# A projection by Strassen's seven products in three passes, with values and output gates turned later

## The reference, cut to what matters

```
xn   = rms_norm(x, g_norm);  proj = xn @ w_in          # 2112 x 1024 x 8200
q,k,v,o,z (1024 each), i,f (4 each), b,c,xc,z_cv (512 each), qx,zx (512 each) = split(proj)
h    = mlstm_chunkwise(q, k/16, v, i + b_i, log_sigmoid(f + b_f))   # 4 heads x 256
y_ml = rms_norm(sigmoid(o) * h, g_head) * silu(z)
y_cv = b * conv3(c * xc) * silu(z_cv)                   # also gives the conv state
y_xa = softmax(qx @ mem_k^T / sqrt(128)) @ mem_v * silu(zx)
out  = rms_norm(x + concat(y_ml, y_cv, y_xa) @ w_out, g_final)
```

## Time and profile before

| | us |
|---|---|
| median of 3 runs | 2346.0 (2344.82 to 2348.57) |
| the profiled execution | 2348.49 |
| its span, first to last instruction | 2346.7 |
| prep | 0 to 69.0 |
| project, first to last matmul | 69.0 to 1572.1 |
| attend | 1577.4 to 1882.9 |
| recur | 1882.9 to 2346.7 |
| PE busy | 2276.5 (97%) |
| mean granted clock of TensorE | 0.988 |

### The profile page before, as it was taken

How to read it: one execution, slowest core, us unless ns; L and a number is a source line. 1 busy time by engine, 2 the same in 40 slices (tenths; PEclk the granted TensorE clock), 3 DMA queues, 4 the chain that set the end, 5 groups by cost and what they waited for, 6 DMA issues and landing times. The chain is left out here.

```text
span 2346.7 us, 30090 instructions
## 1 busy us (share of the span) xinstructions
PE 2276.5 (97%) x11540; PEld 2021.2 (86%) x11540; DVE 694.2 (30%) x1524; ACT 435.4 (19%) x1000; POOL 177.9 (8%) x301
## 2 busy tenths in 40 slices
PE   7999999999999999999999999998999969999998
PEld 4899999999999999888888888987877858888885
DVE  7202323323001011011010333224334435555554
ACT  7110000001111111111111101113333222332231
POOL 0001000000100002300000000000000022222220
PEclk9999999999999999999999999999999989999999
DMA  7321101101122122222121255226445457677653
GB/s 271 86 81 42 51 8 52 45 14 66 49 85 90 49 84 83 53 78 75 57 83 45 83 75 58 99 75 213 162 123 158 153 155 218 186 221 210 197 164 82
DMA packets 237740, 245.40 MB, mean 105 GB/s; under 512 B 51000, under 2 KB 186976, under 8 KB 237616
## 3 DMA queue, kind: packets, MB, share of 16 engines
q1 hardware_dynamic: 193600, 164.17, 24.8%
q10 hardware_dynamic: 37648, 66.54, 8.4%
q0 software_dynamic: 6368, 12.96, 1.9%
HBM read 158.76 MB, written 84.85 MB: 104 GB/s over the span
## 5 line engine op out<-in xcount | busy, mean ns | idle before, releaser
L575 PE MATMUL bank<-xh,wh 128*128 128x424 f32 (+1 forms) x1640 | 581.0, 354 | 6.2 <-DVE wl L537 5.7
L577 PE MATMUL bank<-xh,wl 128*128 128x424 f32 (+1 forms) x1640 | 580.7, 354 | 0.0
L576 PE MATMUL bank<-xl,wh 128*128 128x424 f32 (+1 forms) x1640 | 580.6, 354 | 0.0
L575 PEld LDWEIGHTS bank<-xh,wh 128*128 128x128 f32 x1640 | 308.7, 188 | 16.0 <-DVE wl L537 8.2
L575 PE MATMUL bank<-wh,xh 128*128 128x512 f32 x816 | 317.6, 389 | 1.6 <-DVE wl L537 0.9
L576 PE MATMUL bank<-wl,xh 128*128 128x512 f32 x816 | 317.4, 389 | 0.0
L577 PE MATMUL bank<-wh,xl 128*128 128x512 f32 x816 | 317.4, 389 | 0.0
L576 PEld LDWEIGHTS bank<-xl,wh 128*128 128x128 f32 x1640 | 309.4, 189 | 5.5
L577 PEld LDWEIGHTS bank<-xh,wl 128*128 128x128 f32 x1640 | 308.9, 188 | 4.5
L545 DVE CAST wh<-raw 128x512 fp32r<-128x512 f32 (+1 forms) x136 | 55.8, 412 | 797.0 <-PE bank L577 792.1
L575 PEld LDWEIGHTS bank<-wh,xh 128*128 128x128 f32 x816 | 153.2, 188 | 34.0 <-DVE wl L537 2.3
(11 more groups left out here) (249 smaller groups left out, 2437.3 us busy)
## 6 DMA issues: line engine op xcount, KB each, us to landing
raw<-in_w_in SPq DMA_DIRECT2D x128, 256.0 KB, 4.0
scr_tm<-stage ACTq DMA_DIRECT2D x96, 256.0 KB
raw<-scr_qk SPq DMA_DIRECT2D x16, 1024.0 KB, 6.7
area<-scr_tm SPq DMA_DIRECT2D x32, 512.0 KB, 5.9
scr_qk<-stage ACTq DMA_DIRECT2D x48, 212.0 KB
xin<-in_x_prompt SPq DMA_DIRECT2D x16, 512.0 KB, 4.2
x_res<-in_x_prompt SPq DMA_DIRECT2D x16, 512.0 KB, 3.4
scr_acc<-x_res SPq DMA_DIRECT2D x16, 512.0 KB, 5.6
```

Of the source, the lines that this page charges most:

```text
L575: pe.matmul(out, ah, bh, start=(k == 0), stop=False)
L576: pe.matmul(out, ah, bl, start=False, stop=False)
L577: mm = pe.matmul(out, al, bh, start=False, stop=(k == KD - 1))
```

## The change

The projection's token-major and chunked groups are replaced by one scheme. The 2112 tokens are taken in three passes of 704 (two halves of 352). Every job but the gates is a *pair*: two blocks of 128 output features for one pass. A pair is a 2 x 2 block product (contraction halves by output blocks, times contraction halves by token halves) formed by seven products with sums and differences of the operands (Strassen's scheme in Winograd's form). All results are feature-major. There are 32 pairs and one gate job a pass (`ORDER`), 96 pairs in all.

```diff
+ORDER = [("v", 0), ("gate", 0), ("v", 1), ("u", 0), ("qk", 0), ("cv", 0), ...
+         ("v", 2), ("z", 1), ("v", 3), ("z", 2), ("o", 0), ("z", 3), ("o", 1), ("zx", 0), ... ("qx", 0), ("qx", 1)]
+        def product(q, b, out, first):
+            pe.wait_ge(S["w_low"], CN.block[q] + b + 1)
+            if place(q) == 0:
+                pe.wait_ge(S["x_low"], 7 * (q // UNITS_A_PASS) + b + 1)
+            for k in range(4):
+                pe.matmul(out, wh[:, b, k, :], xh[:, b, k, :], start=(first and k == 0), stop=False, ...)
+                pe.matmul(out, wh[:, b, k, :], xl[:, b, k, :], start=False, stop=False, ...)
+                m = pe.matmul(out, wl[:, b, k, :], xh[:, b, k, :], start=False, stop=(k == 3), ...)
+            m.then_inc(S["product"], 1)
...
+            b, g, h = (bank[3 * (r % 2) + x][:, 0:HALF] for x in range(3))
+            wait(pe, S["out_act"], r - 1)
+            wait(pe, S["out_dve"], 3 * (r - 1))
+            product(q, 0, b, True)
+            product(q, 1, g, True)
+            pe.wait_ge(S["snap"], 3 * r + 1)
+            product(q, 2, b, False)
+            product(q, 3, h, True)
+            pe.wait_ge(S["snap"], 3 * r + 3)
+            product(q, 4, b, False)
+            pe.wait_ge(S["snap"], 3 * r + 2)
+            product(q, 5, g, False)
+            pe.wait_ge(S["out_dve"], 3 * r + 2)
+            product(q, 6, b, False)
+            turn(q)
```

Products run into three PSUM banks that hold running sums; ACT takes three copies of intermediate sums (`snap`), DVE adds them to get three of the four result blocks, and ACT copies the fourth. POOL forms four combinations of weight blocks, ACT rounds the seven operands to high halves, DVE subtracts:

```diff
+            pool.tensor_tensor(wt[:, 0], b12, b11, ALU.subtract).then_inc(S["t_ready"], 1)
+            pool.wait_ge(S["t_ready"], 4 * r + 1)
+            pool.tensor_tensor(b12, b22, b12, ALU.subtract).then_inc(S["t_ready"], 1)
+            pool.tensor_tensor(wt[:, 1], b22, wt[:, 0], ALU.subtract).then_inc(S["t_ready"], 1)
+            pool.wait_ge(S["t_ready"], 4 * r + 3)
+            pool.tensor_tensor(wt[:, 2], b21, wt[:, 1], ALU.subtract).then_inc(S["t_ready"], 1)
...
+        for q in range(N):                       # ACT; DVE has the same loop with w_low, x_low, norm
+            for i in range(7):
+                evacuate(q, i)
+                post(q - 1, i)
+                w_high(q + 1, i)
+                x_high(q + 1, i)
+                if i == 3:
+                    squares(q)
+                    back(q)
+            gate_chain(q)
```

Queues change as follows. All stores of results move from ACT's queue to SP's, in SP's loop behind the load of the job after next; v, o and z go to `scr_vo` and `scr_z`. The chain of the gates moves from POOL's queue to ACT's, at jobs 3 to 27 of the last pass (`at = q - G`), behind the splits of the job:

```diff
+            if at == 27:
+                act.wait_ge(S["gate_stored"], 16 * gate_stores[0])
+                for name, row in (("gc", "g"), ("wsc", "ws"), ("emc", "em")):
+                    for h in range(H):
+                        act.dma_start(columns[name][:, h, :], w[row][h, 0:T].rearrange("(c t) -> t c", t=P)).then_inc(S["columns_loaded"], 16)
```

The stores of the convolution's state now stand on SP after the store of the last job, and the loads that end the block behind them:

```diff
+        load(2)
+        sp.dma_start(gx[:, :], row_bcast(g_norm[0], P)).then_inc(S["gain_loaded"], 16)
+        sp.dma_start(gh[:, :], g_head[0].rearrange("(f p) -> p f", p=P)).then_inc(S["small_loaded"], 16)
         ...
+        for q in range(N):
+            if q + 2 < N and q:
+                load(q + 2)
+            load_x(q)
+            store(q - 1)
+        store(N - 1)
         for j in range(4):
             sp.dma_start(conv_prompt[...], cnew_p[:, j, :]).then_inc(S["conv_state_stored"], 16)
             sp.dma_start(conv_sample[...], cnew_s[:, j, :, :]).then_inc(S["conv_state_stored"], 16)
-        sp.wait_ge(S["conv_state_stored"], 8 * 16)
```

```diff
+                for j in range(8):
                     update(t, j)
+                    if j in (2, 4):
+                        turn_vo(t + 1, j // 2 - 1)
+                    if j == 6 and front_of(t) is not None:
+                        unit_turn_vo(front_of(t))
...
+        def y_gate(t):
+            wait(dve, S["z_loaded"], 16 * t)
+            for i in range(2):
+                zi = z[:, 4 * i:4 * i + 4, :]
+                dve.wait_ge(S["y_turned"], 2 * t + i + 1)
+                dve.tensor_tensor(zi, bank[3 + i].ap().rearrange("p (f t) -> p f t", f=4), zi,
+                                  ALU.mult).then_inc(S["y_gated"], 1)
```

More of the change, by code:

```diff
@@ L206, in of_memory, with moves, moved @@
[L206 to L217, removed]
+        return P if u < 2 else ROW_TILES[0][u - 2][1]
+    def moves(u):
+        return 1 if u < 2 else len(pieces(0, u - 2))
+    def moved(u):
+        return sum(moves(x) for x in range(u + 1))
@@ L219, in _ @@
     @block.sync
     def _(sp):
[L221 to L231, removed]
+        for u in range(NR):
+            if u >= SLOTS:
+                sp.wait_ge(S["x_turned"], u - SLOTS + 1)
+            src = mem_rows[u] if u < 2 else x_rows(x_prompt, x_sample, 0, u - 2)
+            sp.dma_start(xin[:rows(u), u % SLOTS, :], src).then_inc(S[f"x_loaded{u % SLOTS}"], 16)
+            if u == 0:
@@ L485, in _, with outputs, before_write, turned_before @@
+    def outputs(q):
+        p = CN.pair[q] % 2
+        return [[stage[:, p, n, HALF * half:HALF * (half + 1)] for half in range(2)] for n in range(2)]
+    def before_write(eng, q, n):
+        r = CN.pair[q]
+        p = r % 2
+        wait(eng, S[f"stored{p}{n}"], CN.stored[q][n])
+        wait(eng, S["post"], CN.posted[q - 1][0] if q else 0)
+    def turned_before(s, i):
+        return sum(len(pieces(x + 1, j)) for x in range(s + 1) for j in range(6) if (x, j) < (s, i))
     @block.sync
@@ new lines, in gates @@
+        def gates(q):
+            s = q // UNITS_A_PASS
+            wait(pe, S["x_back0"], sum(len(pieces(x, i)) for x in range(1, s + 1) for i in range(6)))
+            wait(pe, S["x_back1"], sum(len(pieces(x, i)) for x in range(1, s + 1) for i in range(6)))
+            for b, parts in ((0, ((6, A11), (7, S1))), (1, ((6, A12),)), (2, ((7, A22),))):
+                pe.wait_ge(S["w_low"], CN.block[q] + b + 1)
+                for where, x in parts:
+                    for k in range(4):
+                        pe.matmul(bank[where][:, 0:HALF], wh[:, b, k, :], xh[:, x, k, :], start=(b == 0 and k == 0), stop=False)
+                        m = pe.matmul(bank[where][:, 0:HALF], wh[:, b, k, :], xl[:, x, k, :], start=False,
+                                      stop=(b > 0 and k == 3))
+                m.then_inc(S["product"], 1)
@@ L805, in _, with w_high @@
-    @block.gpsimd
-    def _(pool):
+        def w_high(q, b):
+            if b >= blocks(q):
+                return
+            if JOBS[q][1] == "gate":
+                act.wait_ge(S["gd_ready"], 1)
+            elif b in (0, 3, 5):
+                act.wait_ge(S[f"raw_loaded{CN.pair[q] % 2}"], CN.loaded[q])
+            else:
+                act.wait_ge(S["t_ready"], made(q, b))
+            wait(act, S["product"], CN.free[q][b])
+            act.activation(halves(q, b)[0], source(q, b), ACT.Copy).then_inc(S["w_high"], 1)
@@ new lines, in tanh, with post @@
+        def tanh(q, n):
+            kind, r = JOBS[q][1], CN.pair[q]
+            act.wait_ge(S["out_dve"], 3 * r + 3)
+            act.wait_ge(S["out_act"], r + 1)
+            wait(act, S["post"], CN.posted[q][0])
+            dst = thc[:, :] if kind == "cv" else th[n]
+            act.activation(dst, stage[:, r % 2, n, :], ACT.Tanh, scale=0.5).then_inc(S["tanh_ready"], 1)
+        def post(q, i):
+            if q < 0:
+                return
+            kind = JOBS[q][1]
+            if kind in ("z", "zx") and i in (0, 2):
+                tanh(q, 1 - i // 2)
+            if kind == "cv" and i == 0:
+                tanh(q, 1)
@@ L1733, in _ @@
         scores(0)
[L1734 removed]
+        turn_vo(0, 0)
+        turn_vo(0, 1)
         for t in range(NT):
```

1320 lines of the change are left out of this document (753 added, 567 removed).

## The result

The changed kernel takes 2401.0 us (median of 4, 2396.4 to 2407.5) against 2346.2 for the one before, run beside it: 1.0235 of it, interval 1.0209 to 1.026. It is 2.3% slower. The forecast was 2275, range 2228 to 2345, with 17% for slower.

What follows compares the result with a forecast made beforehand. It took PE, busy 97% of the span, as the bound, through matmul count and length in the projection. From 2348.5, -142.5 to the projection's end, +35.7 gap and +34.5 recurrence gave 2276.2, stated as 2275 us; range 2228 to 2345.

Steps and rivals of the forecast that it cites:

- The matmuls: Projection: 8064 matmuls of 352 columns at 161 ns (bounds 158 to 167), 1298.3 us; the old ones 1491.8 by their spacings.
- Rival (a): Projection: the weight load, 188 ns as a floor, sets the matmul spacing; total 2500 us, slower; chance 9%.
- The feeders: Projection: ACT, DVE and POOL each need under PE's 13.5 us a pair, so 0 lost; upper end 96 us.
- small loads: Projection's first pair: DVE waits for late small loads before its first addition; PE waits about 4.7 us (0 to 10).
- boundaries: Between the projection's passes: splitting x operands as well makes DVE late; 7 us for two (0 to 15).
- Rival (b): Projection: product 6's addition or a snapshot late in most pairs, 0.75 to 2 us each, total 2347 to 2465; chance 10%.
- The gap: Ahead of attend: state stores and later loads queue on SP behind the last store; 41 us instead of 5.3, +35.7.
- The column loads: Projection: twelve gate column loads hold ACT 16 us in one piece; PE loses 13.7 us.
- the rest of the chain: Projection: the gates' other small DMAs, moved to ACT's queue ahead of weight splits; PE loses about 7 us.
- The recurrence: Recurrence: 16 more transposes a tile (28.0 us), unit transposes 3.5, slower start 3; +34.5 us in all.
- Start: Before the projection: shorter prep brings the first product to 64.4 from 68.99 us, -4.6 (-12 to +3).

Runs made afterwards that it cites:

- the run with rows: Changed kernel with the convolution's state turned on TensorE and stored as rows of 512 bytes, same eight DMAs at the same place on SP: 2347.1 us (0.9989 of before).

## Why the prediction was wrong

**The matmuls: right.** 159.8 ns against the 161 taken, and 8064 of them. Rival (a), the weight load as the bound, is out: LDWEIGHTS of 128 columns follow at 160 ns, and PEld's busy share in the projection is 91% at this faster spacing. The rule that the prediction cites from the Trainium skill, "Perfetto Trace Analysis", section Identifying the Most-Contended Engine, to judge TensorE by MFU and the busy share of LDWEIGHTS, would have spoken against the step; here a share of 98% was no bound. The records of loads are 188 to 192 ns long at a spacing of 226.5, of 190.5 and of 159.8 ns alike, so at the last they overlap. (The prediction gives the plain fp32 loads of the recurrence 190 ns too; the trace has 198. Its argument stands.)

**The feeders: the step that failed.** The prediction said that DVE makes "7 low halves at 0.69", that "the tightest chain is product 6", and put 0 on it. Two things in it were wrong. The price came from rows in which POOL did nothing (the earlier trace rows has POOL at 0.00 in both stretches of the projection), and the change puts 5 us of POOL beside each pair: 812 and 1036 ns, and 1.98 us for a step of a post that takes 0.89 alone. And the slack of product 6 was checked by busy time (6.5 us of 13.5), not by what stands ahead of the addition in DVE's order. The prediction's own condition, "where DVE is not behind", fails behind every post; where no post stands ahead, nearly nothing is lost. Of the 110.6 us, 16.3 are the small loads' and the boundaries', forecast as 11.7; the other 94.3 stand where the forecast has a zero, 0.98 us a pair on average. Rival (b) had the place and the size (0.75 to 2 us a pair), though it saw it in most pairs and it is in about half of them; it had 10%. The Trainium skill, "SBUF — State Buffer", section SBUF: two separate sides, says that VectorE and GpSimd share one pair of ports under an exclusive lock held for a whole instruction, which VectorE needs when both operands are in SBUF or in a two-port mode. The runs agree: steps with two SBUF operands are lengthened, the additions from PSUM are not (517 and 522 ns with and without POOL), and the long low halves end a fixed 0.55 us after POOL's instruction. L997, a tensor by a scalar, is lengthened too (1588 ns against 648); which mode it runs in no trace shows.

**The gap: right direction, half its size.** The forecast took 25 us of issue and 9 for the loads with their landing. The issue took 36, w_out's loads held the same queue for 17 and those of `work` for 3, and the last of these landed 16 us after its issue. The cause is in the stores of single elements, as the run with rows shows. In the gap there are 9488 packets of 4 bytes, nearly all of them the state's, with a recorded mean of 110 ns each (median 9; the fifth over 100 ns holds 93% of the time). That is 65.5 us for each of 16 engines, but such records overlap (with all the others they come to 1.16 of the stretch), so it is no share of the gap; and the same stores were recorded at 57 ns in the middle of the kernel before and at 79 behind its last product. The columns' 24,576 elements, read from DRAM one by one on ACT's queue, took 8.8 ns each. So it is elements *written* to DRAM one by one that were dear here, and not those read. The Trainium skill, "DMA: Bandwidth & Descriptors", section Specifications, says that below 512 bytes a DMA engine reads, modifies and writes. The rows of 512 bytes fit it (54 us gained), but with 72 packets in place of 9216 they would gain by the count alone too; and the 4-byte column loads, which the Trainium skill's sentence doesn't set apart, were cheap.

**The column loads: right in kind, too small by half.** 19.8 us in the pair where they stand, 13.7 forecast, and 22 given back by moving them: they held ACT for 20.6 us and not for 16. They and the rest of the chain were put at 20.7.

**The recurrence: right, a little high.** A pair of tiles is 56.59 us, 3.93 above, as 32 transposes at 109 ns and a unit's four give (3.94). Eight pairs are 31.4. By difference the start got 6 us shorter, not 3 longer. PE's waits for data in its first 62 us fell from 13.3 to 10.0 us, and the first unit's loads took SP 10.5 us where they took 14.8; that the one comes from the other isn't shown.

**Start and boundaries.** The turning of the keys began at 60.75, where it was 62.64, but from there to the first product it is 8.2 us and no longer 6.4; of the 4.6 us nothing came. The boundaries cost 5.4 and 6.2 us at product 6, where 3.5 were said; I didn't separate what POOL adds there.

So of the miss of 126 us, 94 are the feeders and 33 the gap with its written elements; the smaller differences all but cancel. With both mended and the column loads on POOL's queue the time is 2224.9, under the forecast of 2275 and just under its range: the gap of 41 and the columns' stall of 13.7, which the forecast had counted in, became 16.8 and nothing.

What stays open: how much of the 110 us is the holding of DVE's steps itself and how much a wait for POOL's `wt` through ACT's order; the runs take both away together. Why a tenth of the written elements were recorded above 428 ns, where the median is 9, isn't shown either, nor whether the direction alone makes them dear.

## What to carry to other kernels

When a change puts an idle engine to work, price its neighbours' instructions from rows in which that engine was busy; and not from their average alone: here an instruction beside POOL took up to twice its time and one without POOL its old time. Test the slack of each hand-over by what stands ahead of it in program order, not by busy shares. Put what the next matmul waits for ahead of what only the next block needs. Small strided stores are paid by everything that uses the DMA engines until they have drained: turn them into rows, or issue them where nothing follows for tens of microseconds.

## What the runs showed of the hardware beyond the forecast

- DVE steps with operands in SBUF are lengthened by POOL beside them by up to a factor of 2.4 (704 elements: tensor by tensor 886 to 1981 ns, tensor by scalar 648 to 1588); those that read PSUM are not (522 and 517). They are held to the end of POOL's instruction: 144 of the 148 low halves over 1 us end 0.55 us after one.
- Elements of 4 bytes written to DRAM from SP's queue were recorded at 110, 79 and 57 ns on average in three places, with a median of 9 in each; elements of 4 bytes read from DRAM on ACT's queue at 8.8. On POOL's queue both are recorded as packets of up to 256 bytes.
- Such stores slow the issue of other queues' DMAs: ACT's seven gate stores took 15.0 us where 2.6 us were taken by the seven of the next group. They slow other packets too: 1024-byte ones took 114 ns on average beside them, 58 without.
- 128 x 128 weight loads run at 160 ns each beside 352-column matmuls with PE full; a share of 98% at 190 ns was not a limit. Each load's record is some 190 ns long whatever the spacing.
